# A hybrid encoder layer with experts: the first token tile's router and half of the first gather placed inside the output projection

## The chip, the cores and the metric

The kernel runs on one core of one Trainium2 chip. The metric is the device time of one execution in microseconds. In the code `pe` is TensorE, `dve` VectorE, `act` ScalarE, `pool` GpSimd, and `sp` the queue on SyncE that issues nearly all DMAs.

## What is computed

One encoder layer for 256 tokens of width 1024, all in float32. The first half mixes tokens (gated linear attention and softmax attention) and ends in an output projection; the second half sends every token to 4 of 32 experts. What matters here:

```python
h = h + concat([o_gla, o_att]) @ w_out                 # output projection, residual
n = rms_norm(h, ffn_norm_g)
logits = n @ w_router + b_router                       # 32 experts
top_val, top_idx = top_k(logits, 4); gates = softmax(top_val)
for each expert e, over the tokens that chose it:
    a = x_e @ w1[e] + b1[e]                            # w1[e]: 1024 x 2048
    act = min(a_glu, 7) * sigmoid(1.702 * a_glu) * (clip(a_lin, -7, 7) + 1)
    y += gate * (act @ w2[e] + b2[e])                  # w2[e]: 1024 x 1024
out = rms_norm(h + y, final_norm_g)
```

The weights of the experts are 32 x 12.58 MB = 403 MB; each is read once.

## The kernel before

**Tiles.** The 256 tokens are two tiles of 128 partitions (`t` = 0, 1); the residual `h` lies in SBUF as `h[:, t, 0:1024]`. An expert takes its tokens in a block of at most 64 (`CAP`). Which token goes to which place of the block is a 128 x 64 matrix per tile, `onehot[:, t, :]`, already scaled by the token's 1/rms. The expert's input `xg` must have the model dimension on the partitions.

**Order.** There is no scheduler: each engine runs its instructions in the order in which its block is written, and waits on semaphores (`S....`). Around the change the order is this.

1. The output projection on TensorE: `out_gla(t, nb, ks)` (L1456) is one 128x512 matmul per `k`, for tile `t` and half `nb` of the 1024 columns. When `k == 3` is done it counts `h_ps`. VectorE then adds the residual, `add_h(t, nb)` (L973, counts `h_done`), ScalarE squares the result for the norm (L590), and `turn_h(t, half)` (L1431) transposes the new `h` with four 128x128 turns, which VectorE or ScalarE copy into `hT` (L977, L595).
2. The router of a tile: `router_round(t, half)` (L1439, four 32-column matmuls each), a copy on ScalarE (L600), `router_sum(t)` (L1447), then on VectorE `choose(t)` (L990 to L995: logits, top values, the mask `chosen`), a matmul that counts places (L1501 for tile 0, L1506 for tile 1), and `first_mask(t)` (L1014, L1016), which writes `onehot[:, t, :]`.
3. The first gather, for expert 0: `first_gather(half, t)` (L1531) has `onehot` stationary (64 columns) and `h` moving (256 columns), two matmuls each. The rows that come out have the tokens on the partitions, so they are copied to SBUF (L1069 on VectorE for half 0, L617 on ScalarE for half 1), turned by `turn_first` (L1540) and multiplied by the norm's gain into `xg` (`half_out`, L1076). `keep_busy(n)` (L1487) is n matmuls whose result nobody reads.
4. The experts: TensorE multiplies `xg` by w1 (L1657, 8 matmuls per chunk of 2 MB, four chunks), then the activation, then w2 (L1701, two chunks). `start_hidden` (L1481) puts b1 into the accumulators.

**The weight ring.** SBUF has eight slots of 2 MB, plus three chunks that are loaded early elsewhere. A slot is refilled when TensorE has counted `chunk_used` for it. Slot 7 holds the projection's weights `w_out_gla` until all four `h_ps` are counted; its first chunk is issued after that (L345). So before expert 0 starts, everything that can be loaded has been loaded, and the next load waits for expert 0's first chunk.

The order of TensorE in the last part of the projection is written out by hand:

```python
out_gla(1, 0, range(4))
turn_h(0, 0)
turn_h(0, 1)
out_gla(1, 1, range(3))
turn_h(1, 0)
out_gla(1, 1, range(3, 4))
```

Of the kernel before, what the change touches and what calls it, by code (L numbers as in the profile page):

```python
# [120 lines left out]
def encoder_layer(nc, x, w_in, w_out, w_router, w1, b1, w2, b2, gate_w, columns, rows, final_g,  # L121
                  c_keep, c_front, later, split, out):
    ctx = ExitStack()
    with ctx:
# [28 lines left out]
        class Carve:  # L153
# [113 lines left out]
            onehot_ready onehot_first half_gathered half_rows half_turned half_xg gathered rows_done turned_ps xg_ready glu_ready sig_ready hid_ready combined  # L267
# [202 lines left out]
        def _(act):  # L470
# [133 lines left out]
            turned_out(0, 1, 1)  # L604
            square(1, 0)
            turned_out(1, 0, 7)
            router_parts(0)
# [7 lines left out]

            act.wait_ge(S.gathered, 1)
            nc.scalar.activation(rows_sb[:, SEQ:2 * SEQ], bank[6][:, 0:SEQ], ACT.Copy).then_inc(S.rows_done, 1)  # L617
# [68 lines left out]
        def _(dve):  # L686
# [313 lines left out]
            add_h(0, 0)  # L1000
            add_h(0, 1)
            mean_square(0)
            add_h(1, 0)
            turned_out(0, 0, 0)
            add_h(1, 1)
            turned_out(1, 1, 4)
            mean_square(1)
            dve.wait_ge(S.marks, 2)
            choose(0)
            choose(1)  # L1010

            def first_mask(t):
# [5 lines left out]
                    .then_inc((S.onehot_first, S.onehot_ready)[t], 1)  # L1018

# [39 lines left out]
            def gathered_out(n):  # L1059

                dve.wait_ge(S.turned_ps, n + 1)
# [5 lines left out]
            def half_rows_out():  # L1067
                dve.wait_ge(S.half_gathered, 1)
                nc.vector.tensor_copy(rows_sb[:, 0:SEQ], bank[3][:, 0:SEQ]).then_inc(S.half_rows, 1)  # L1069

            def half_out(half, b):

                n = KD // 2
                runs = W1_RUN // GROUPS
                dve.wait_ge((S.half_turned, S.turned_ps)[half], 1)
                nc.vector.tensor_tensor(xg[:, half * n * CAP:(half + 1) * n * CAP].rearrange("p (j r c) -> p j r c", j=GROUPS, c=CAP),  # L1076
                                        bank[b][:, SEQ:2 * SEQ].rearrange("p (r j c) -> p j r c", j=GROUPS, c=CAP),
                                        ffn_pairs[:, half * n:(half + 1) * n].rearrange("p (j r o) -> p j r o", j=GROUPS, o=1)
                                        .broadcast_to([P, GROUPS, runs, CAP]), ALU.mult).then_inc((S.half_xg, S.xg_ready)[half], 1)
# [91 lines left out]
        def _(pe):  # L1171
# [313 lines left out]
            def keep_busy(n):  # L1485
                for _ in range(n):
                    mm(bank[3][:, 0:P], ident, h[:, 0, 0:P], start=True, stop=True)  # L1487
# [285 lines left out]
```

## Time and profile before

| | us |
|---|---|
| median of 3 runs | 1052.62 |
| lowest and highest | 1050.64, 1052.72 |
| span of the profiled execution | 1047.4 |

The page and the answers of the trace show one profiled execution. PE is TensorE's matmuls, PEld its loads of stationary operands (a float32 matmul has two records of each, a turn has one), SPq the queue on SyncE. In the page's part on groups the columns are: line, engine, operation, written tile<-read tiles, shapes, count, then busy time and mean ns of one, then idle time ahead and what ended it. A row by stage has the stretch, its length, the busy time of PE, PEld, VectorE, ScalarE and GpSimd with counts, the granted TensorE clock (1.00 is 2.4 GHz, 0.50 is 1.2 GHz), the busy share of the DMA engines and GB/s. A row of the chain of work that ended last, or of the timeline, starts with its start and its length in us; in a PE row of either, the length reaches to the end of the last of the merged matmuls.

TensorE is busy for 1002.2 us of the span, VectorE for 223.0, ScalarE for 133.0; the DMA engines moved 421.48 MB at a mean of 402 GB/s.

### The profile page before, as it was taken

To read this page: it belongs to the slowest core of one execution; us is meant where nothing else is said; L and a number is where in the kernel's file an instruction comes from. 1 tells how busy PE (TensorE), PEld (TensorE's weight loads), DVE (VectorE), ACT (ScalarE), POOL (GpSimd) and SP (SyncE) were. 2 spreads that over 40 slices of the span, in tenths; PEclk is the share of its full clock that TensorE was granted. 3 is DMA by queue.
4 is the path that set the end of the run, shared out by engine and by line. 5 is a ranking of instruction groups with operands and counts; after the bars stand their busy time and mean duration, and the time that the engine had idled before them with its cause. 6 is when DMAs were issued, how large, how long until landed. Compare 5 with 4: busy or idle time off the path is not lost.

```text
span 1047.4 us, 11293 instructions
## 1 busy us (share of the span) xinstructions
PE 1002.2 (96%) x4739; PEld 429.8 (41%) x4739; DVE 223.0 (21%) x519; ACT 133.0 (13%) x262; POOL 13.4 (1%) x18
## 2 busy tenths in 40 slices
PE   8999999999999999989999989899999999999996
PEld 7646444444444444433343433333333333443332
DVE  5385331111111111111111111011111111110112
ACT  1154121111100000111110100011111010010112
POOL 0010100000000000000000000000000000000000
PEclk9999999999999999999999999999999999999999
DMA  9927969999999999999999999999999999999995
GB/s 356 283 80 316 407 254 430 427 428 430 425 427 428 427 429 425 429 433 432 434 429 432 427 435 426 436 430 430 432 430 437 427 437 430 425 427 428 428 423 224
DMA packets 26964, 421.48 MB, mean 402 GB/s; under 512 B 4368, under 2 KB 4752, under 8 KB 6864
## 3 DMA queue, kind: packets, MB, share of 16 engines
q1 hardware_dynamic: 26640, 420.68, 95.3%
q8 instruction: 29, 0.48, 0.2%
q10 hardware_dynamic: 288, 0.27, 0.1%
q14 instruction: 7, 0.06, 0.0%
HBM read 419.89 MB, written 1.05 MB: 402 GB/s over the span
## 4 chain that ended last, share of the span: by engine, by line
PE 68%; DMA 28%; DVE 1%; ACT 1%; POOL 0%; issue 0%; SPq 0%; DVEq 0%
PE bank L1657 30%; DMA ring<-in_w_dram 27%; PE bank L1701 15%; PE bank L1569 4%; PE bank L1550 3%; PE bank L1213 2%; PE bank L1683 1%; PE bank L1456 1%; PE bank L1287 1%; DMA ring<-in_w_in_dram 1%; PE bank L1384 1%; PE bank L1558 1%; PE bank L1481 1%; PE bank L1617 1%; PE bank L1256 1%; PE bank L1692 0%
## 5 line engine op out<-in xcount | busy, mean ns | idle before, releaser
L1657 PE MATMUL bank<-ring,work 128*64 128x512 f32 x2000 | 453.9, 606 | 30.9 <-DMA ring<-in_w_dram 30.9
L1657 PEld LDWEIGHTS bank<-ring,work 128*64 128x64 f32 x2000 | 175.1, 138 | 289.6 <-issue 235.0
L1701 PE MATMUL bank<-ring,work 128*64 128x512 f32 x992 | 219.7, 595 | 0.2
L1092 DVE TENSOR_SCALAR work<-bank 128x512 f32<-128x512 f32 x31 | 21.5, 692 | 641.7 <-PE bank L1657 641.7
L1701 PEld LDWEIGHTS bank<-ring,work 128*64 128x64 f32 x992 | 68.7, 137 | 129.4 <-issue 124.5
L627 ACT ACTIVATE bank<-work 128x512 f32<-128x512 f32 x31 | 18.6, 601 | 496.7 <-DVE work L1092 496.7
L1569 PE MATMUL bank<-work 64*128 64x512 f32 x256 | 63.6, 615 | 0.7 <-ACT work L664 0.7
L1550 PE MATMUL bank<-h,work 128*64 128x512 f32 x248 | 60.0, 593 | 0.0
L640 ACT ACTIVATE work<-bank 128x512 f32<-128x512 f32 x31 | 18.5, 597 | 214.5 <-PE bank L1701 214.5
L1569 PEld LDWEIGHTS bank<-work 64*128 64x128 f32 x256 | 22.0, 186 | 41.8 <-issue 40.2
L1062 DVE TENSOR_TENSOR work<-bank,ffn_pairs 128x512 f32<-128x512 f32 x31 | 21.5, 692 | 72.3 <-PE bank L1558 72.3
L1550 PEld LDWEIGHTS bank<-h,work 128*64 128x64 f32 x248 | 23.5, 137 | 30.0 <-issue 30.0
L1683 PEld LDWEIGHTS bank<-ckeep,work 128*128 128x128 f32 x124 | 17.3, 209 | 24.7 <-DVE work L1098 23.2
L622 ACT ACTIVATE work<-bank 128x512 f32<-128x512 f32 x31 | 18.5, 597 | 46.8 <-DVE work L1098 43.6
L1683 PE MATMUL bank<-ckeep,work 128*128 128x128 f32 x124 | 23.2, 309 | 1.1 <-DVE work L1098 1.1
L632 ACT ACTIVATE work<-bank 128x512 f32<-128x512 f32 x31 | 18.5, 597 | 28.9 <-PE bank L1683 28.8
L440 POOL TENSOR_TENSOR stat<-stat 128x1 f32<-128x1 f32 (+2 forms) x8 | 9.7, 1212 | 964.7 <-DVE stat L696 940.2
L1095 DVE SCALAR_TENSOR_TENSOR work<-work 128x512 f32<-128x512 f32 x31 | 21.4, 692 | 1.1
L1098 DVE TENSOR_TENSOR work<-work,bank 128x512 f32<-128x512 f32 x31 | 21.3, 686 | 1.1
L1093 DVE TENSOR_SCALAR work<-bank 128x512 f32<-128x512 f32 x31 | 21.1, 681 | 0.0
L1481 PE MATMUL bank<-biases,sel 96*64 96x512 bf16 x128 | 20.0, 389 | 0.0
L1558 PE MATMUL bank<-ckeep,work 128*128 128x128 f32 x124 | 20.0, 284 | 0.0
(217 smaller groups left out, 520.7 us busy)
## 6 DMA issues: line engine op xcount, KB each, us to landing
ring<-in_w_dram SPq DMA_DIRECT2D x48, 4096.0 KB, 29.8
ring<-in_w_dram SPq DMA_DIRECT2D x90, 2048.0 KB, 20.2
ring<-in_w_in_dram SPq DMA_DIRECT2D x8, 1168.0 KB, 17.5
ring<-in_w_dram SPq DMA_DIRECT2D x6, 1024.0 KB, 34.1
work<-in_w_dram SPq DMA_DIRECT2D x2, 2048.0 KB, 14.7
ring<-in_w_out_dram SPq DMA_DIRECT2D x2, 1024.0 KB, 11.0
ring<-in_w_out_dram SPq DMA_DIRECT2D x1, 2048.0 KB, 17.2
h<-in_x_dram SPq DMA_DIRECT2D x2, 512.0 KB, 3.7
```

The lines of the kernel that those rows point to most:

```text
L1062: nc.vector.tensor_tensor(xg.rearrange("p (h r c) -> p h r c", h=GROUPS, c=CAP), bank[2][:, :].rearrange("p (r h c) -> p h r c", h=GROUPS, ...
L1092: nc.vector.tensor_scalar(glu, bank[2][:, :], LIMIT, None, ALU.min).then_inc(S.glu_ready, 1)
L1093: nc.vector.tensor_scalar(lin, bank[5][:, :], LIMIT, -LIMIT, ALU.min, ALU.max).then_inc(S.dve_step, 1)
L1095: nc.vector.scalar_tensor_tensor(lin, lin, 1.0, glu, ALU.add, ALU.mult).then_inc(S.dve_step, 1)
L1098: nc.vector.tensor_tensor(lin, lin, bank[2][:, :], ALU.mult).then_inc(S.hid_ready, 1)
L1481: mm(bank[(2, 5)[g]][j * CAP:(j + 1) * CAP, :], sel, of_group(b1_parts, g, j), start=True, stop=False, skip_group_check=True)
L1550: last = mm(bank[6][j * CAP:(j + 1) * CAP, :], onehot[:, t, :], h[:, t, j * 512:(j + 1) * 512], start=t == 0, stop=t == TILES - 1, skip_gr ...
L1558: last = nc.tensor.transpose(bank[2][:, r * P:(r + 1) * P], apart[:, :, r], ident)
L1569: last = mm(bank[Y[i]][:, :], gatedT[j * CAP:(j + 1) * CAP, t, :], res[j * CAP:(j + 1) * CAP, :], start=start, stop=stop, skip_group_check ...
L1657: last = mm(bank[(2, 5)[g]][j * CAP:(j + 1) * CAP, :], xg[:, k * CAP:(k + 1) * CAP], of_group(row_of(chunk, r, 2 * FF), g, j), start=False ...
L1683: last = nc.tensor.transpose(bank[5][:, r * P:(r + 1) * P], apart[:, :, r], ident)
L1701: last = mm(bank[6][j * CAP:(j + 1) * CAP, :], hidT[:, r, s * CAP:(s + 1) * CAP], row_of(chunk, r, D)[:, j * 512:(j + 1) * 512], start=s = ...
```

## The change

Tile 0's router no longer waits for the end of the projection. On TensorE, `turn_h(0, ...)` goes ahead of the last two matmuls of `out_gla(1, 0)`; `router_round(0, ...)`, `router_sum(0)`, `turn_h(1, 0)` and the counting matmul of tile 0 go between the four matmuls of `out_gla(1, 1)`. VectorE and ScalarE are reordered to match: `choose(0)` and `first_mask(0)` stand ahead of `add_h(1, 1)`.

The first gather is written the other way round: `h` (every fourth column, 128 of them) is stationary and `onehot` (64 columns) moves, four matmuls in place of two for each half and tile. Its result has the model dimension on the partitions already, so both copies (L1069, L617) and both `turn_first` (L1540) are gone. Tile 0's two parts stand inside tile 1's router, around `turn_h(1, 1)`; tile 1's two parts stand directly ahead of expert 0. All six `keep_busy` matmuls are gone.

```diff
@@ -602,9 +602,9 @@
             square(0, 0)
             square(0, 1)
             turned_out(0, 1, 1)
+            router_parts(0)
             square(1, 0)
             turned_out(1, 0, 7)
-            router_parts(0)
             square(1, 1)
             router_parts(1)
...
                     .then_inc(S.wexp_done, 1)
-
-            act.wait_ge(S.gathered, 1)
-            nc.scalar.activation(rows_sb[:, SEQ:2 * SEQ], bank[6][:, 0:SEQ], ACT.Copy).then_inc(S.rows_done, 1)
 
             def rows_out(n):
                 act.wait_ge(S.gathered, n + 1)
@@ -997,18 +994,6 @@
...
             dve.wait_ge(S.pairs_in, 16 * W1_RUN * W1_RUN)
-            add_h(0, 0)
-            add_h(0, 1)
-            mean_square(0)
-            add_h(1, 0)
-            turned_out(0, 0, 0)
-            add_h(1, 1)
-            turned_out(1, 1, 4)
-            mean_square(1)
-            dve.wait_ge(S.marks, 2)
-            choose(0)
-            choose(1)
-
...
+            add_h(0, 0)
+            add_h(0, 1)
+            turned_out(0, 0, 0)
+            mean_square(0)
+            add_h(1, 0)
+            dve.wait_ge(S.marks, 2)
+            choose(0)
+            first_mask(0)
+            add_h(1, 1)
+            turned_out(1, 1, 4)
+            mean_square(1)
+            choose(1)
+            first_mask(1)
...
-            def half_rows_out():
-                dve.wait_ge(S.half_gathered, 1)
-                nc.vector.tensor_copy(rows_sb[:, 0:SEQ], bank[3][:, 0:SEQ]).then_inc(S.half_rows, 1)
-
             def half_out(half, b):
 
                 n = KD // 2
-                runs = W1_RUN // GROUPS
-                dve.wait_ge((S.half_turned, S.turned_ps)[half], 1)
-                nc.vector.tensor_tensor(xg[:, half * n * CAP:(half + 1) * n * CAP].rearrange("p (j r c) -> p j r c", j=GROUPS, c=CAP),
-                                        bank[b][:, SEQ:2 * SEQ].rearrange("p (r j c) -> p j r c", j=GROUPS, c=CAP),
-                                        ffn_pairs[:, half * n:(half + 1) * n].rearrange("p (j r o) -> p j r o", j=GROUPS, o=1)
-                                        .broadcast_to([P, GROUPS, runs, CAP]), ALU.mult).then_inc((S.half_xg, S.xg_ready)[half], 1)
+                dve.wait_ge((S.half_gathered, S.gathered)[half], 1)
+                nc.vector.tensor_tensor(xg[:, half * n * CAP:(half + 1) * n * CAP].rearrange("p (r c) -> p r c", c=CAP),
+                                        bank[b][:, 0:n * CAP].rearrange("p (r c) -> p r c", c=CAP),
+                                        ffn_pairs[:, half * n:(half + 1) * n].rearrange("p (r o) -> p r o", o=1)
+                                        .broadcast_to([P, n, CAP]), ALU.mult).then_inc((S.half_xg, S.xg_ready)[half], 1)
...
-            first_mask(0)
-            first_mask(1)
-            half_rows_out()
             half_out(0, 3)
+            half_out(1, 6)
             tables()
-            half_out(1, 6)
...
             pe.wait_ge(S.glaT_v, 1)
             out_gla(0, 0, range(4))
             out_gla(0, 1, range(4))
-            pe.wait_ge(S.glaT_a, 1)
-            out_gla(1, 0, range(4))
-            turn_h(0, 0)
-            turn_h(0, 1)
-            out_gla(1, 1, range(3))
-            turn_h(1, 0)
-            out_gla(1, 1, range(3, 4))
-
...
 
+            def first_gather(half, t):
+
+                if half == 0:
+                    pe.wait_ge((S.onehot_first, S.onehot_ready)[t], 1)
+                apart = h[:, t, half * 512:(half + 1) * 512].rearrange("p (m r) -> p m r", r=W1_RUN)
+                for r in range(W1_RUN):
+                    last = mm(bank[(3, 6)[half]][:, r * CAP:(r + 1) * CAP], apart[:, :, r], onehot[:, t, :],
+                              start=t == 0 and r == 0, stop=t == TILES - 1, skip_group_check=True)
+                if t == TILES - 1:
+                    last.then_inc((S.half_gathered, S.gathered)[half], 1)
+
+            pe.wait_ge(S.glaT_a, 1)
+            out_gla(1, 0, range(2))
+            turn_h(0, 0)
+            turn_h(0, 1)
+            out_gla(1, 0, range(2, 4))
             pe.wait_ge(S.wr_done, 1)
-            def keep_busy(n):
-                for _ in range(n):
-                    mm(bank[3][:, 0:P], ident, h[:, 0, 0:P], start=True, stop=True)
-
             router_round(0, 0)
             router_round(0, 1)
+            out_gla(1, 1, range(1))
+            router_sum(0)
+            out_gla(1, 1, range(1, 3))
+            turn_h(1, 0)
+            pe.wait_ge(S.chosen_done, 1)
+            mm(bank[1][:, 0:EXPERTS], before_b, chosen[:, 0, :], start=True, stop=True).then_inc(S.rank_ps, 1)
+            out_gla(1, 1, range(3, 4))
             router_round(1, 0)
+            first_gather(0, 0)
             turn_h(1, 1)
-            router_sum(0)
-            keep_busy(2)
+            first_gather(1, 0)
             router_round(1, 1)
             router_sum(1)
             start_hidden(0)
-
-
-            pe.wait_ge(S.chosen_done, 1)
-            mm(bank[1][:, 0:EXPERTS], before_b, chosen[:, 0, :], start=True, stop=True).then_inc(S.rank_ps, 1)
-            pe.wait_ge(S.hT_a, 2)
+            pe.wait_ge(S.hT_v, 2)
             mm(bank[7][:, 0:EXPERTS], ones_b, chosen[:, 0, :], start=True, stop=False)
             mm(bank[4][:, 0:EXPERTS], ones_b, chosen[:, 0, :], start=True, stop=False)
             pe.wait_ge(S.chosen_done, 2)
...
-            RUNS = W1_RUN // GROUPS
-
-            def first_gather(half, t):
-                if half == 0 and t == 0:
-                    keep_busy(4)
-                pe.wait_ge((S.onehot_first, S.onehot_ready)[t], 1)
-                for j in range(GROUPS):
-                    last = mm(bank[(3, 6)[half]][j * CAP:(j + 1) * CAP, 0:RUNS * P], onehot[:, t, :],
-                              h[:, t, half * 512:(half + 1) * 512].rearrange("p (m r) -> p m r", r=W1_RUN)[:, :, j * RUNS:(j + 1) * RUNS], start=t == 0, stop=t == TILES - 1, skip_group_check=True)
-                if t == 1:
-                    last.then_inc((S.half_gathered, S.gathered)[half], 1)
-
-            def turn_first(half):
-                pe.wait_ge((S.half_rows, S.rows_done)[half], 1)
-                apart = rows_sb[:, half * RUNS * P:(half + 1) * RUNS * P].rearrange("p (m r) -> p m r", r=RUNS)
-                for r in range(RUNS):
-                    last = nc.tensor.transpose(bank[(3, 6)[half]][:, (RUNS + r) * P:(RUNS + r + 1) * P], apart[:, :, r], ident)
-                last.then_inc((S.half_turned, S.turned_ps)[half], 1)
...
-                    if first and c == 0:
-                        turn_first(1)
                     if first and c == 1:
...
-            first_gather(0, 0)
             first_gather(0, 1)
-            first_gather(1, 0)
-            turn_first(0)
             first_gather(1, 1)
```

The `first_gather` of the diff is used for expert 0 alone; the later gathers stay as they were. Two waits of the later experts count one less, since the first gather no longer counts `rows_done` and `turned_ps`.

TensorE's order from the last matmuls of the projection to expert 0's first chunk, before (L1456 is the projection, L1431 the turns, L1439 and L1447 the router, L1487 the unread matmuls, L1531 the gather, L1540 `turn_first`, L1657 expert 0):

```order
127 L1456 MATMUL bank<-ring,work 128x512 x3
128 L1431 MATMUL bank<-ckeep,h 128x128 x4
129 L1456 MATMUL bank<-ring,work 128x512
130 L1439 MATMUL bank<-work,wr_sb 32x128 x12
131 L1431 MATMUL bank<-ckeep,h 128x128 x4
132 L1447 MATMUL bank<-ckeep,work 128x32
133 L1487 MATMUL bank<-h,ckeep 128x128 x2
134 L1439 MATMUL bank<-work,wr_sb 32x128 x4
```

And now (L1447 is here the projection, L1422 the turns, L1430 and L1438 the router, L1491 the counting matmul, L1473 the gather):

```order
127 L1447 MATMUL bank<-ring,work 128x512 x2
128 L1430 MATMUL bank<-work,wr_sb 32x128 x8
129 L1447 MATMUL bank<-ring,work 128x512
130 L1438 MATMUL bank<-ckeep,work 128x32
131 L1447 MATMUL bank<-ring,work 128x512 x2
132 L1422 MATMUL bank<-ckeep,h 128x128 x4
133 L1491 MATMUL bank<-work,ckeep 128x32
134 L1447 MATMUL bank<-ring,work 128x512
135 L1430 MATMUL bank<-work,wr_sb 32x128 x4
136 L1473 MATMUL bank<-work,h 128x64 x4
137 L1422 MATMUL bank<-ckeep,h 128x128 x4
138 L1473 MATMUL bank<-work,h 128x64 x4
```

Eight narrow router matmuls, the router's sum and the count moved ahead of the projection's last matmul, and four gather matmuls ahead of the last turn (row 137).

TensorE's last rows ahead of expert 0's first chunks, before:

```order
143 L1531 MATMUL bank<-h,work 64x256 x6
144 L1540 MATMUL bank<-ckeep,work 128x128 x2
145 L1531 MATMUL bank<-h,work 64x256 x2
146 L1657 MATMUL bank<-ring,work 64x512 x8
147 L1540 MATMUL bank<-ckeep,work 128x128 x2
148 L1657 MATMUL bank<-ring,work 64x512 x8
```

And now (L1504, L1505 count tile 1's places, L1636 is expert 0):

```order
144 L1504 MATMUL bank<-work,ckeep 128x32
145 L1505 MATMUL bank<-work,ckeep 128x32
146 L1473 MATMUL bank<-work,h 128x64 x8
147 L1636 MATMUL bank<-ring,work 64x512 x16
148 L1510 MATMUL bank<-ckeep,work 128x128 x2
```

The turns between gather and expert are gone, and eight gather matmuls with 128 stationary columns stand where eight with 64 stood.

## Rows read from the trace of the kernel before

**Rows 1.** The page: the profiled span, and the costliest group.

```profile
span 1047.4 us, 11293 instructions
...
L1657 PE MATMUL bank<-ring,work 128*64 128x512 f32 x2000 | 453.9, 606 | 30.9 <-DMA ring<-in_w_dram 30.9
```

**Rows 2.** By stage: two stretches of the experts.

```profile
260.00:500.00 240.00, 235.59 (x1114) 95.96 (x1112) 40.46 (x90) 24.00 (x45) 0.00 (x0) 0.99 1.01 428
...
750.00:1000.00 250.00, 234.98 (x1090) 92.70 (x1088) 36.67 (x82) 21.98 (x42) 0.00 (x0) 0.98 1.00 429
```

**Rows 3.** The chain of work that ended last: two early experts, first DMA piece.

```profile
186.29 7.07 PE bank L1701 x32
...
212.62 7.07 PE bank L1701 x32
...
437.71 30.85 DMA ring<-in_w_dram
```

**Rows 4.** By stage, 1 us each: where the DMA engines stop and resume.

```profile
138.00:139.00 1.00, 1.00 (x12) 0.56 (x8) 0.02 (x1) 0.00 (x0) 0.00 (x0) 1.00 0.64 270
139.00:140.00 1.00, 0.92 (x8) 0.42 (x6) 0.40 (x1) 0.00 (x0) 0.00 (x0) 1.00 0.00 0
...
144.00:145.00 1.00, 1.00 (x6) 0.52 (x6) 0.27 (x1) 0.00 (x0) 0.00 (x0) 1.00 0.00 0
145.00:146.00 1.00, 1.00 (x8) 0.41 (x5) 0.92 (x9) 0.00 (x0) 0.00 (x0) 1.00 1.00 213
```

**Rows 5.** The chain of work that ended last, 115 to 150 us.

```profile
131.21 0.86 PE bank L1456 x2
132.07 0.79 PE bank L1439 x24
132.86 0.66 PE bank L1431 x4
...
134.29 0.47 PE bank L1439 x8
...
137.87 1.08 PE bank L1531 x8
...
139.46 0.51 PE bank L1540 x2
...
140.57 3.62 PE bank L1657 x16
```

**Rows 6.** Timeline, 131 to 142 us: the same stretch by instruction.

```profile
132.10 0.69 DVE L973 TENSOR_TENSOR h<-bank,h 128x512 f32<-128x512 f32 x1 [3.46 <-PE bank L1456]
...
133.54 0.69 DVE L977 COPY work<-bank 128x512 f32<-128x512 f32 x1 [0.75 <-PE bank L1431]
...
135.56 0.25 DVE L990 SCALAR_TENSOR_TENSOR work<-bank,stat,work 128x32 f32<-128x32 f32 x1
...
137.19 0.31 DVE L1016 TENSOR_SCALAR work<-ckeep,work,stat 128x64 f32<-128x64 f32 x1
...
138.98 0.42 DVE L1069 COPY work<-bank 128x256 f32<-128x256 f32 x1 [1.47 <-PE bank L1531]
...
140.00 0.42 DVE L1076 TENSOR_TENSOR work<-bank,ffn_pairs 128x256 f32<-128x256 f32 x1 [0.60 <-PE bank L1540]
```

**Rows 7.** Timeline: loads of stationary operands, 32 columns, 128 together, 128 strided.

```profile
132.00 0.59 PEld L1439 LDWEIGHTS bank<-work,wr_sb 128*32 128x32 f32 x24 [0.76 <-issue]
...
136.71 0.97 PEld L1487 LDWEIGHTS bank<-h,ckeep 128*128 128x128 f32 x8
...
185.54 0.56 PEld L1558 LDWEIGHTS bank<-ckeep,work 128*128 128x128 f32 x4
```

**Rows 8.** By stage, 1 us each: the granted clock around short and long idle stretches.

```profile
136.00:137.00 1.00, 0.59 (x9) 0.47 (x8) 0.89 (x8) 0.89 (x3) 0.00 (x0) 1.00 0.92 393
...
467.00:468.00 1.00, 0.00 (x0) 0.00 (x0) 0.00 (x0) 0.00 (x0) 0.00 (x0) 1.00 0.99 426
...
469.00:470.00 1.00, 1.00 (x4) 0.24 (x2) 0.00 (x0) 0.00 (x0) 0.00 (x0) 0.50 0.84 360
```

More of the change, by code:

```diff
@@ L266, in encoder_layer @@
             parts_ps part_sb_done logit_ps top_done wexp_done chosen_done rank_ps count_ps tables_done gateT_ps gateT_sb extra_done
-            onehot_ready onehot_first half_gathered half_rows half_turned half_xg gathered rows_done turned_ps xg_ready glu_ready sig_ready hid_ready combined
+            onehot_ready onehot_first half_gathered half_xg gathered rows_done turned_ps xg_ready glu_ready sig_ready hid_ready combined
             gated_ready gatedT_ps gatedT_sb hidT_ps hidT_sb res_ready chunk_used
@@ L1059, in gathered_out @@
             def gathered_out(n):
-                dve.wait_ge(S.turned_ps, n + 1)
+                dve.wait_ge(S.turned_ps, n)
                 nc.vector.tensor_tensor(xg.rearrange("p (h r c) -> p h r c", h=GROUPS, c=CAP),
@@ L1554, in turn_rows @@
             def turn_rows(n):
-                pe.wait_ge(S.rows_done, n + 1)
+                pe.wait_ge(S.rows_done, n)
                 apart = rows_sb.rearrange("p (m r) -> p m r", r=W1_RUN)
```

## The prediction

> **What bounds the kernel now.** First the page. TensorE is busy 96% of the span, and the group of expert matmuls has 30.9 us of idle time ahead of it, all put down to the DMA of weights [rows 1]. The share hides which of the two limits, so next come the stages: from 260 to 500 us and from 750 to 1000 us the DMA engines are full (shares 1.01 and 1.00) at 428 and 429 GB/s [rows 2]. An expert's 12.58 MB at 429 GB/s take 29.3 us. TensorE needs less: in the chain two early experts stand 212.62 - 186.29 = 26.33 us apart, without a wait [rows 3]. So the DMA engines are the slower of the two by 3.0 us an expert; TensorE lives on what was loaded ahead until 437.71 us, where the chain first passes through a transfer [rows 3].
>
> The span is therefore the moment at which the DMA engines start to work without a break, plus the rest of the weights at 429 GB/s, plus a tail. That moment is in the rows of 1 us: the transfers end between 138 and 139 us, there are none from 139 to 145, and they are full again in the row from 145 [rows 4]. The ring is full and waits for expert 0's first chunk to be used. The chain says when: the chunk's matmuls start at 140.57 and take 3.62, to 144.19 us [rows 5]; the first bytes come about 1 us later. From then on a chunk takes 2.1 MB / 429 GB/s = 4.9 us to load and about 4.1 us to use, so the queue stays fed. **What the change is worth is how much earlier or later expert 0's first chunk is used, and nothing else**; TensorE's savings behind that point only make it wait longer for the ring.
>
> **The path to that point, before.** The projection's last matmul ends at 132.06 [rows 5]; add at 132.10; turn at 132.86; copy at 133.54; router matmuls at 134.29; logits on VectorE at 135.56; tile 1's `onehot` is done at 137.19 + 0.31 = 137.50 [rows 5, 6]. This chain is tile 1's router. Tile 0's runs beside it and is not in it. Then: gather from 137.8, copy at 138.98, turn at 139.46, gain at 140.00, and the chunk starts at about 140.5 [rows 5, 6]. So 5.4 us from the projection to the mask, and 3.0 us from the mask to the chunk.
>
> **Mask to chunk, after.** The copy (0.42), the turn (0.51) and their handovers go, and so does the wait for the last unread matmuls (137.50 to 137.80). In their place stand eight gather matmuls of tile 1, so 16 records, ahead of the chunk. Their moving operand has 64 columns, their stationary one 128, strided by four. No row shows that form. From below: 128 stationary columns that lie together follow each other every (0.97 - 0.19) / 7 = 0.111 us [rows 7], where 0.19 is the length of one load. The nearest row is the later experts' turn, whose stationary operand is 128 columns strided by four: (0.56 - 0.21) / 3 = 0.117 us [rows 7]. From above I take twice the plain pitch, 0.22, since that row is a turn and has one record per operand, not two. I choose 0.12, by the turn: 16 x 0.12 = 1.92 us, and with 0.06 for the start the chunk begins 1.98 us after the mask. The other branch is shorter: half of the gather (0.96), 0.33 until VectorE sees it, the gain 0.42, 0.06 to TensorE, 1.8 in all; so the matmuls themselves set it, and VectorE's second `half_out` hides beneath the first two chunks. Gain: 3.0 - 2.0 = **1.0 us**.
>
> The Trainium skill, "TensorE: Matmul & The Clock Gate", section "LDWEIGHTS", makes the load a matter of columns alone, columns / 1.2 ns, which is an estimate of 107 ns for 128 columns whatever their stride; the strided row's 0.117 us is above that. By the rule the 16 records would take 1.71 us and the gain would be 1.2 us.
>
> **Projection to mask, after.** Here the change puts work in front of tile 1's chain.
> - Ahead of the projection's last matmul: 16 records of the narrow router at (0.59 - 0.11) / 23 = 0.021 us [rows 7], so 0.34, and an estimated 0.1 to start them; the router's sum, two records, 0.22; the count, about 0.1. Together 0.8 us. The turns and projection matmuls only change places. Nothing waits there: tile 0's logits come at about 129.8, tile 1's took 1.94 us to the finished mask with the count in it (135.56 to 137.50) [rows 6], and TensorE reaches tile 0's count at 131.7. So `h_ps` comes at 132.9, VectorE's add starts there, free since `first_mask(0)` ended near 132.5.
> - Ahead of tile 1's last turn: `router_round(1, 0)`, 0.3, and four gather matmuls, 8 x 0.12 = 0.96. TensorE has issued the projection at 132.7 and reaches the turn at 134.0. The add would allow it at 132.9 + 0.8 = 133.7. So the turn starts at 134.0, where it started at 132.86.
> - The second part of tile 0's gather (0.96) stands behind the turn, where TensorE waits for VectorE's copy anyway: 134.4 to 135.4, and the copy hands over at 134.0 + 0.69 + 0.69 + 0.06 = 135.4. Hidden, but with nothing to spare.
> - Behind that all is as before and moved by the same amount: the mask is done at 137.50 + 1.15 = 138.65. Loss: **1.15 us**. The gain chain of VectorE and GpSimd for the 1/rms is moved too and ends about 0.3 us ahead of the logits.
>
> SyncE's load into slot 7 waits for `h_ps` and is issued 0.8 us later; its transfer ends near 139.5 instead of 138.7, still 4.5 us ahead of the next one. Behind it on that queue stands only the load that waits for the first chunk. Cost: nothing.
>
> **The sum.** 1.15 - 1.0 = +0.15 us: the chunk starts at 140.65 instead of 140.5 and is used at 144.3. The turn taken out behind the first chunk (0.44) helps TensorE alone. The profiled span would go from 1047.4 to 1047.6. The runs are 5.2 us above the span in the median, and that stays: 1052.62 + 0.15 = **1052.8 us**.
>
> **Rivals.**
> - *Tile 1's router isn't pushed back, or the gather goes at its moving columns.* If the four gather matmuls ahead of the turn took 0.5 us (64 of the 128 columns per record) the turn would wait for VectorE alone, at 133.7, and the last 16 records would take 0.9. VectorE's branch would then set the chunk, 1.35 us behind the mask: 138.3 + 1.35 = 139.7, a gain of 0.8; without the 0.8 us in the projection too it would be 1.6. Against it: both rows with 128 stationary columns have 0.11 or more. Time 1051.0 to 1051.8. Chance 0.2.
> - *The strided load is slow.* At 0.22 a record the turn waits until 134.8, the second part of the gather pushes the next router matmuls to 136.9 (2.6 us later than before), and the last 16 records take 3.5: the chunk starts at 143.7, 3.2 us later. The sum turns to slower as soon as a record takes more than 0.115. Time 1055.8; halfway, at 0.16, 1054.1. Chance 0.1.
> - *The clock falls.* The twelve records of unread matmuls are gone and TensorE idles three times for 0.6 us or so between 135.5 and 138.7. Before, the row at 136 us has 0.59 us busy and a full clock; a fall came only behind a longer stop: the row at 467 us is empty, and the row at 469 has 0.50 [rows 8]. No stretch of that kind arises here, which speaks against it. If it falls, the first chunk takes up to twice its 3.62 us: +1.7 to +3.6 us, 1054.5 to 1056.4. Chance 0.12. The Trainium skill's page "TensorE: Matmul & The Clock Gate", section "A second HAM failure mode: psum-queue depth-cycling", says that short idles between groups can be enough to throttle; the 1.00 at 136 us disagrees here.
> - *What bounds is elsewhere*, so that the first chunk's time moves nothing: 1052.6, inside the forecast.
>
> **How the numbers follow.** A measurement of this kernel can tell about 0.2% (2.1 us) from no change; the three runs of before span 2.08 us by themselves. Forecast 0.55; gather by moving columns 0.2; slow load 0.1; clock 0.12; the rest 0.03. Slower by over 0.2% are half of the clock case, a third of the slow load, and scatter, 0.13 in all; faster only the far end of the first rival with scatter, 0.05; within 0.2% is 0.82. Range: from the fastest run of before with a gain of 0.6, 1050.0, to the middle of the slow cases, 1055.1.
>
> **What would show it.** In the profile after: the DMA engines resume at 145 us, give or take 0.5; the mask near 138.7 and the chunk near 140.7; tile 1's last turn near 134.0, behind the gather; 16 strided records in 1.9 us; clock 1.00 from 130 to 145 us; idle time before expert matmuls put down to DMA a little larger. Wrong would be: a mask at 137.5 or earlier, a chunk started well before 140 us, a clock of 0.50 near 140, or a span that moves by another amount than the first chunk does.

## The result

| | median us | runs | ratio to before | 95% interval |
|---|---|---|---|---|
| before | 1051.78 | 4 | 1 | |
| changed | 1055.83 | 4 (1054.54 to 1055.90) | 1.0045 | 1.0032 to 1.0057 |

The change makes the kernel slower by 4 to 5 us: the medians lie 4.05 us apart, and the ratio, which is worked out from the runs and not from the two medians, gives 4.7 us (3.4 to 6.0). I had forecast 1052.8 us and no measurable change. The profiled execution's span went from 1047.4 to 1052.8 us. The page after, span and costliest group (in the changed kernel L1636 is the expert matmul, L1447 the projection, L1430 the router's matmuls, L1422 the turns of `h`, L1473 the new gather):

```profile
span 1052.8 us, 11283 instructions
...
L1636 PE MATMUL bank<-ring,work 128*64 128x512 f32 x2000 | 456.6, 610 | 29.7 <-DMA ring<-in_w_dram 29.7
```

TensorE's idle time for weights hardly moved (30.9 us in [rows 1]), so the loss isn't in the experts' steady part. The stages of 1 us show where it is; they answer [rows 4]:

```profile
139.00:140.00 1.00, 0.66 (x7) 0.16 (x4) 0.82 (x6) 0.99 (x3) 0.00 (x0) 0.60 0.56 238
...
150.00:151.00 1.00, 1.00 (x7) 0.35 (x5) 0.00 (x0) 0.00 (x0) 0.00 (x0) 1.00 0.00 0
151.00:152.00 1.00, 1.00 (x8) 0.50 (x5) 0.00 (x0) 0.00 (x0) 0.00 (x0) 1.00 0.82 180
```

The DMA engines stop about 1 us later than before (the row from 139 us still has 238 GB/s) and resume in the row from 151 us, not in the one from 145. The load that waits for the first chunk is issued at 144.22 us before and at 150.77 us after (SyncE's queue in the timeline, before first, then after):

```profile
144.22 4.40 SPq L345 DMA_DIRECT2D ring<-in_w_dram  x2
```

```profile
150.77 0.33 SPq L345 DMA_DIRECT2D ring<-in_w_dram  x1
```

I call the issue of this load the **restart** and count it from the start of the last part of the projection (116.78 us before, 116.66 after), since that start itself differs between profiles by up to 4 us for reasons ahead of the change. Before it is 144.22 - 116.78 = 27.44 us, after 150.77 - 116.66 = 34.11: **6.67 us later**. The chain of work that ended last shows what fills them; it answers [rows 5]:

```profile
133.05 0.36 PE bank L1430 x8
133.41 2.01 PE bank L1473 x8
135.42 0.44 PE bank L1422 x4
135.86 1.81 PE bank L1473 x8
137.67 0.40 PE bank L1430 x8
...
140.82 3.99 PE bank L1473 x16
144.82 9.38 PE bank L1636 x32
```

Eight records of the gather take 2.0 us, not 0.96, and sixteen take 4.0, not 1.92. The two parts that I had placed as free, around tile 1's last turn, are now in the chain: the turn starts at 135.42 (132.86 before), the next router matmuls at 137.67 (134.29). And the first two chunks take 9.38 us together, where one takes 3.62 at the full clock [rows 5]. The granted clock says why:

```profile
141.00:142.00 1.00, 1.00 (x5) 1.00 (x6) 0.00 (x0) 0.52 (x1) 0.00 (x0) 0.50 0.00 0
...
149.00:150.00 1.00, 1.00 (x6) 0.46 (x4) 0.00 (x0) 0.00 (x0) 0.00 (x0) 0.78 0.00 0
```

From 139.2 to 149.4 us TensorE ran at 1.2 GHz (worked out from the rows at 139 and 149 us, which are part one level and part the other); before, it had 2.4 GHz there. So two of my rivals came true together. Of the 6.67 us, 4.37 lie ahead of the first chunk, which starts 28.16 us behind the projection's start and not 23.79, and 2.30 in the chunk itself: from its start to the next load it is 5.95 us, not 3.65.

### The profile page after: what moved, and what is told of

Its sections match the earlier page's. It is cut to its first block, busy times and chain, and to the rows that moved or that the text cites. A ratio compares the mean times of both kernels' runs of the same rounds, so it can differ in the third digit from the quotient of the medians.

```text
span 1052.8 us, 11283 instructions
## 1 busy us (share of the span) xinstructions
PE 1009.3 (96%) x4739; PEld 436.7 (41%) x4739; DVE 222.9 (21%) x518; ACT 132.7 (13%) x261; POOL 13.4 (1%) x18
## 4 chain that ended last, share of the span: by engine, by line
PE 69%; DMA 27%; DVE 1%; ACT 1%; POOL 0%; issue 0%; SPq 0%; DVEq 0%
PE bank L1636 31%; DMA ring<-in_w_dram 27%; PE bank L1678 15%; PE bank L1548 4%; PE bank L1529 3%; PE bank L1204 3%; PE bank L1660 1%; PE bank L1447 1%; PE bank L1278 1%; PE bank L1375 1%; PE bank L1537 1%; PE bank L1464 1%; PE bank L1473 1%; PE bank L1596 1%; PE bank L1247 1%; DMA ring<-in_w_in_dram 1%
## 5 line engine op out<-in xcount | busy, mean ns | idle before, releaser
L1636 PE MATMUL bank<-ring,work 128*64 128x512 f32 x2000 | 456.6, 610 | 29.7 <-DMA ring<-in_w_dram 29.7
L1636 PEld LDWEIGHTS bank<-ring,work 128*64 128x64 f32 x2000 | 176.5, 139 | 290.1 <-issue 237.8
```

Source lines behind the costliest of these rows:

```text
L1636: last = mm(bank[(2, 5)[g]][j * CAP:(j + 1) * CAP, :], xg[:, k * CAP:(k + 1) * CAP], of_group(row_of(chunk, r, 2 * FF), g, j), start=False ...
```

## The experiments

My first theory: the loss has two causes. One is the load of a stationary operand that is read with a stride; the other is the clock. Rivals: the new form is slow even without a stride; the new order costs by itself; the clock fell because the unread matmuls are gone, or because the slow gather leaves the array idle. Restarts are counted as above, "+" is against the 27.44 us of before. Medians of each group are in the text; ratios are to the kernel before on the same chip and, as above, not exactly the quotients of the medians. The code cuts leave out the parts of an edit that only keep the rest of the program in step.

### Without the stride

```diff
-                apart = h[:, t, half * 512:(half + 1) * 512].rearrange("p (m r) -> p m r", r=W1_RUN)
+                apart = h[:, t, half * 512:(half + 1) * 512].rearrange("p (r m) -> p m r", r=W1_RUN)
```

> The changed kernel with the first gather's stationary operand read as 128 columns that lie together in place of every fourth column (so expert 0 gets the wrong columns of h; work and order are the same). Theory 'stride': the record pitch falls from 0.24 to 0.11-0.12 us, tile 1's last turn starts near 134.1 (was 135.25), the mask is done near 138.7 (140.8), the first chunk starts near 140.8 (144.75). Rival 'two records with 64 moving columns are slow in themselves': pitch stays 0.24 and all those times stay. For the clock: if it fell because the unread matmuls are gone it is still 0.50 near 140-145 us and the DMA engines resume near 147.3 (time about +2.2 us on before); if it fell because the slow gather leaves the array idle it is 1.00 and they resume near 145.4 (time within 0.5 us of before).

Measured: 1051.68 us against 1049.07, ratio 1.0021 (1.0011 to 1.0030); restart 147.69 - 116.77 = 30.92, +3.48 us. The first chain row is a quarter of the gather at the full clock, the second is tile 1's two quarters:

```profile
133.52 1.03 PE bank L1473 x8
...
138.98 3.67 PE bank L1473 x16
```

```profile
138.00:139.00 1.00, 0.23 (x3) 0.13 (x3) 0.61 (x3) 0.98 (x3) 0.00 (x0) 0.77 0.92 393
139.00:140.00 1.00, 1.00 (x5) 1.00 (x5) 0.00 (x0) 0.69 (x1) 0.00 (x0) 0.50 0.64 270
```

At the full clock the stride was the whole cost of a record: 2.01 us for eight became 1.03. But the clock still fell, at 138.5 us, and at 0.50 a record without a stride takes 3.67 / 16 = 0.23 us. So the stride explains the first half of the loss (the restart goes from +6.67 to +3.48), and the clock doesn't need it.

### The unread matmuls back

```diff
             router_round(1, 1)
+            keep_busy(2)
             router_sum(1)
...
+            keep_busy(4)
             first_gather(0, 1)
             first_gather(1, 1)
```

> The changed kernel with the six unread matmuls back: two ahead of router_sum(1), four ahead of first_gather(0, 1). Theory 'the clock fell because they are gone': clock 1.00 throughout, the first chunk takes 3.6 us in place of 5.5, the DMA engines resume near 149.5 in place of 151.3, time 1.7 us below the changed kernel, 2.3 to 3 above before. Rival 'the clock fell because the slow gather leaves the array idle': still 0.50 from about 139 to 149 us, time as the changed kernel or up to 0.5 above it.

Measured: 1055.07 against 1049.07, ratio 1.0060 (1.0044 to 1.0077); restart 150.32 - 116.78 = 33.54, +6.10. The clock stayed full to the end of the gather at 144.98 us and fell 0.4 us behind it:

```profile
139.00:140.00 1.00, 0.67 (x6) 0.13 (x4) 0.90 (x6) 0.99 (x2) 0.00 (x0) 1.00 0.64 270
...
141.00:142.00 1.00, 1.00 (x7) 1.00 (x6) 0.00 (x0) 0.63 (x1) 0.00 (x0) 1.00 0.00 0
...
146.00:147.00 1.00, 1.00 (x4) 0.26 (x2) 0.89 (x8) 0.00 (x0) 0.00 (x0) 0.50 0.00 0
```

With the strided gather the unread matmuls save 0.6 us at most: the fall only comes later, in the first chunk. Neither of my two expectations for the clock came out, since it was neither full throughout nor low from 139 us on.

### The order alone, and the form alone

The changed kernel's order with the old form of the gather (`onehot` stationary, copy, turn), without unread matmuls:

```diff
+                for j in range(GROUPS):
+                    last = mm(bank[(3, 6)[half]][j * CAP:(j + 1) * CAP, 0:RUNS * P], onehot[:, t, :],
...
-                apart = h[:, t, half * 512:(half + 1) * 512].rearrange("p (m r) -> p m r", r=W1_RUN)
```

> The changed kernel's order with the first gather in its old form (onehot stationary, copy, turn, gain). Theory 'the form costs, the order costs little': h_ps as in the changed kernel (133.1), the turn starts near 133.9, the mask is done near 138.5, the first chunk starts near 140.9, used at 144.6 if the clock stays at 1.00: time +0.5 us on before; +2.3 if the clock falls. Rival 'the order is what costs': the first chunk starts at 143 or later with the old form too.

Measured: 1052.08 against 1049.07, ratio 1.0024 (1.0015 to 1.0034); restart 147.36 - 116.75 = 30.61, +3.17. The mask of tile 1 is done at 138.62 us, 1.12 later than before. The rest is the clock: the first chunk takes 5.43 us.

```profile
141.90 5.43 PE bank L1653 x16
```

```profile
144.00:145.00 1.00, 1.00 (x4) 0.23 (x1) 0.00 (x0) 0.00 (x0) 0.00 (x0) 0.50 0.00 0
```

The kernel before with the new form only, in its old order, its unread matmuls kept:

```diff
-                    last = mm(bank[(3, 6)[half]][j * CAP:(j + 1) * CAP, 0:RUNS * P], onehot[:, t, :],
...
+                    last = mm(bank[(3, 6)[half]][:, r * CAP:(r + 1) * CAP], apart[:, :, r], onehot[:, t, :],
```

> The kernel before in its old order, with unread matmuls, and only the first gather in its new form. Mask at 137.5 as before; then 32 records. Theory 'stride': 32 x 0.24 = 7.7 us, the first chunk starts near 145.6, the DMA engines resume near 150.3 with a full clock: time +5.0 us on before. Rival (my prediction's pitch of 0.12): 3.9 us, the chunk starts at 141.8, time +1.3.

Measured: 1054.46 against 1049.07, ratio 1.0056 (1.0039 to 1.0072); restart 150.89 - 116.73 = 34.16, +6.72. All 32 records stand in the chain, at 7.46 / 32 = 0.233 us each, and the clock falls in the middle of them, at 142.4 us, though unread matmuls stand directly ahead:

```profile
137.83 7.46 PE bank L1523 x32
145.29 9.03 PE bank L1642 x32
```

```profile
140.00:141.00 1.00, 1.00 (x6) 1.00 (x5) 0.00 (x0) 0.00 (x0) 0.00 (x0) 1.00 0.00 0
...
142.00:143.00 1.00, 1.00 (x6) 1.00 (x6) 0.00 (x0) 0.00 (x0) 0.00 (x0) 0.69 0.07 16
...
144.00:145.00 1.00, 1.00 (x6) 1.00 (x5) 0.00 (x0) 0.00 (x0) 0.00 (x0) 0.50 0.00 0
```

Here TensorE counts as busy in every row from 137 us on, and loads stationary operands throughout the gather, and the clock falls all the same.

### The load by itself

Batches of unread matmuls at the kernel's start, each 16 records, behind 24 warming ones:

```diff
+            def by(r, n=P):
+                return h0.rearrange("p (m r) -> p m r", r=r)[:, 0:n, 0]
+            for _ in range(8):
+                mm(bank[0][:, 0:64], h0[:, 0:P], ones[:, 0:64], start=True, stop=True)
+            for _ in range(8):
+                mm(bank[0][:, 0:64], by(2), ones[:, 0:64], start=True, stop=True)
+            for _ in range(8):
+                mm(bank[0][:, 0:64], by(4), ones[:, 0:64], start=True, stop=True)
...
```

> The changed kernel with batches of unread matmuls at its start, behind 24 warming ones: 8 float32 matmuls each (16 records) with 128 stationary columns that lie together, every 2nd, every 4th, every 8th; then 64 stationary columns together and every 4th; then every 4th with 128 and with 256 moving columns; then 16 turns with the operand together and every 4th. Theory 'a strided stationary operand loads at half speed in a matmul, not in a turn': pitch 0.11-0.12 together, 0.24 at every stride from 2 on, 0.06 and 0.12 for 64 columns, 0.24 with 128 and with 256 moving columns, 0.11 and 0.12 for the turns. Rival 'only a stride of 16 bytes or more is slow': every 2nd stays at 0.12.

The loads, in order: 128 columns together; every 2nd; 4th; 8th; 64 columns together and every 4th; every 4th with 128 and with 256 moving columns; turns, together and every 4th (timeline, start and length of the batch):

```profile
13.63 1.87 PEld L1193 LDWEIGHTS bank<-work,h 128*128 128x128 f32 x16
15.42 1.96 PEld L1195 LDWEIGHTS bank<-work,h 128*128 128x128 f32 x16
17.30 3.81 PEld L1197 LDWEIGHTS bank<-work,h 128*128 128x128 f32 x16
21.02 3.90 PEld L1199 LDWEIGHTS bank<-work,h 128*128 128x128 f32 x16
25.04 1.78 PEld L1201 LDWEIGHTS bank<-work,h 128*64 128x64 f32 x16
26.70 2.02 PEld L1203 LDWEIGHTS bank<-work,h 128*64 128x64 f32 x16
28.83 3.81 PEld L1205 LDWEIGHTS bank<-work,h 128*128 128x128 f32 x16
32.55 3.83 PEld L1207 LDWEIGHTS bank<-h 128*128 128x128 f32 x16
36.28 1.90 PEld L1209 LDWEIGHTS bank<-ckeep,h 128*128 128x128 f32 x16
38.15 2.01 PEld L1211 LDWEIGHTS bank<-ckeep,h 128*128 128x128 f32 x16
```

The granted clock has to be read beside these lengths:

```profile
17.00:18.00 1.00, 1.00 (x8) 1.00 (x8) 0.00 (x0) 0.00 (x0) 0.00 (x0) 1.00 0.98 400
18.00:19.00 1.00, 1.00 (x6) 1.00 (x6) 0.00 (x0) 0.00 (x0) 0.00 (x0) 0.89 0.98 402
...
22.00:23.00 1.00, 1.00 (x6) 1.00 (x6) 0.00 (x0) 0.00 (x0) 0.00 (x0) 0.50 1.02 430
...
34.00:35.00 1.00, 1.00 (x6) 1.00 (x6) 0.00 (x0) 0.00 (x0) 0.00 (x0) 1.00 1.09 190
```

At the full clock a matmul's 128 columns cost 0.12 us a record when they lie together or when every second is taken, and 0.24 us at every 4th, also with 128 and 256 moving columns. **The turn is indifferent**: 0.12 with and without the stride, both at the full clock. That is the row that I had gone by. My expectation said that every 2nd would be slow; there the rival, "only 16 bytes or more", was right.

The clock fell in this run too, at 18.8 us, 1.5 us into the first batch of every 4th column, with TensorE busy in every row from 5 us on. It came back at 29.0 us, as the batch with 128 moving columns had begun, and with 128 and 256 moving columns the same stride kept the full clock for the 7 us up to 36 us. So the stride alone isn't what brings the clock down; here it fell only with 64 moving columns. This is one profile. So the batch of every 8th and both batches of 64 columns ran at 0.50. There 128 columns that lie together cost 0.23 us a record as well (e1_contig), so the 0.24 of every 8th doesn't show a cost of that stride, and the two batches of 64 columns (0.11 together, 0.13 at every 4th) say nothing of them at the full clock.

### Both causes taken away

The changed kernel's order and form, with the model dimension stored in another order so that the stationary columns lie together (`x`, `w_in`, `w_out`, the router and the gains permuted alike, and the gain loaded in one piece, not in 16; the turns of the later experts read columns that lie together too), and the unread matmuls back:

```diff
+    apart = np.arange(D).reshape(2, P, W1_RUN).transpose(0, 2, 1).reshape(-1)
...
-        "x": np.asarray(x)[0],
+        "x": np.asarray(x)[0][:, apart],
...
-                apart = h[:, t, half * 512:(half + 1) * 512].rearrange("p (m r) -> p m r", r=W1_RUN)
+                apart = h[:, t, half * 512:(half + 1) * 512].rearrange("p (r m) -> p m r", r=W1_RUN)
```

> The changed kernel's order and form, with the model dimension stored in another order (x, w_in, w_out, the router and the gains permuted alike), so that the first gather's 128 stationary columns lie together, and with the six unread matmuls back. Theory 'two causes, stride and clock': pitch 0.12, mask near 138.8, first chunk near 140.9, clock 1.00 to the end of the first chunk, DMA engines resume near 145.5: time within 0.5 us of before. If the unread matmuls don't hold the clock even with the quick gather: 0.50 in the first chunk, resume near 147.5, time +2 us.

Measured: 1050.27 against 1051.15, ratio 0.9988 (0.9979 to 0.9998); restart 148.68 - 120.69 = 27.99, +0.55. The clock stays full through the gather and the first chunks:

```profile
143.28 1.73 PE bank L1469 x16
145.01 7.07 PE bank L1638 x32
```

```profile
145.00:146.00 1.00, 1.00 (x7) 0.44 (x8) 0.88 (x4) 0.00 (x0) 0.00 (x0) 1.00 0.06 16
```

The mask of tile 1 is done at 142.84 us, 22.15 behind the projection's start where before has 20.72: +1.43. The chunk starts 2.17 us behind the mask in place of 3.07: -0.90. Together that is +0.53, where my sum was 1.15 - 1.0 = +0.15. The ratio is a little below 1 although the restart is 0.55 us later. The kernel differs from before in the early loads and the later turns as well, so I don't read a gain of the change into it.

The order alone with the unread matmuls back; the edit to e3_order is that of e2_unread:

> The changed kernel's order with the old form of the gather, as in e3_order, and the six unread matmuls back. Theory 'in e3_order 1.1 us was the order and the rest the clock': clock 1.00 through the first chunk, mask near 138.6, chunk started near 141.2 and used near 144.9, DMA engines resume near 145.8: time +0.7 us on before, 2.3 below e3_order. Rival 'the order alone costs 3 us': the resume stays near 148.

Measured: 1051.47 against 1050.78, ratio 1.0007 (0.9997 to 1.0017); restart 145.31 - 117.13 = 28.18, +0.74. The first chunk takes the usual time, at a full clock:

```profile
141.67 3.62 PE bank L1658 x16
```

```profile
141.00:142.00 1.00, 1.00 (x7) 0.40 (x8) 0.83 (x4) 0.29 (x1) 0.00 (x0) 1.00 0.00 0
```

The mask is done 1.15 us later than before and the chunk starts 0.75 us later. Next to e6_apart, the same order with the quick form (+0.53), this gives what the new form is worth when nothing slows it: 0.2 us.

### Only the unread matmuls taken out

```diff
             router_sum(0)
-            keep_busy(2)
...
-                if half == 0 and t == 0:
-                    keep_busy(4)
```

> The kernel before without its six unread matmuls, nothing else. Theory 'the clock fell because they are gone': the granted clock is 0.50 from about 137 us, the gather's records and the first chunk take longer, the DMA engines resume near 148 in place of 145.1, time +2.5 to +3 us. Rival 'the clock depends on the new gather and order alone': clock 1.00, time 0.3 us below before (the gather starts at 137.5 in place of 137.8).

Measured: 1050.31 against 1051.15, ratio 0.9988 (0.9975 to 1.0001); restart 146.52 - 118.58 = 27.94, +0.50. The clock does fall, at 139.7 us, but it is back at 143.1, with nearly all of the first chunk (142.75 to 146.49 us) at the full clock. Both of my expectations for the time were wrong: the unread matmuls hold the clock, but in the order of before that is worth 0.5 us in the profile and nothing that the runs can tell.

```profile
141.00:142.00 1.00, 1.00 (x6) 0.60 (x6) 0.27 (x1) 0.00 (x0) 0.00 (x0) 0.50 0.00 0
...
143.00:144.00 1.00, 1.00 (x6) 0.34 (x4) 0.26 (x2) 0.98 (x2) 0.00 (x0) 0.94 0.00 0
144.00:145.00 1.00, 1.00 (x7) 0.35 (x5) 0.00 (x0) 0.48 (x1) 0.00 (x0) 1.00 0.00 0
```

### Does the end follow the first chunk?

```diff
             first_gather(1, 1)
+            for _ in range(4):
+                mm(bank[1][:, :], ident, h[:, 0, 0:512], start=True, stop=True)
```

> The kernel before with four unread matmuls of 512 columns (3.4 us) directly ahead of expert 0's first chunk. Theory 'the end follows the first chunk one for one': the chunk starts at 143.9, the DMA engines resume near 148.6, time +3.4 us. Rival 'the ring has slack, the bound lies elsewhere': time within 0.5 us of before.

Measured: 1053.43 against 1050.78, ratio 1.0029 (1.0018 to 1.0041), which is 3.0 us (1.9 to 4.3); restart 147.88 - 116.80 = 31.08, +3.64; span 1051.0 against 1047.4, +3.6. One for one, within the scatter. The chain has the four unread matmuls (L1712) and, behind them, the chunk at its usual length:

```profile
140.59 3.63 PE bank L1712 x8
144.22 3.63 PE bank L1657 x16
```

### A better order

The order of before with the quick form, that is with the model dimension stored as in e6_apart: three quarters of the gather ahead of the first chunk, the last one behind it, and four unread matmuls in place of six. The cut is against the kernel before:

```diff
             first_gather(0, 0)
             first_gather(0, 1)
             first_gather(1, 0)
-            turn_first(0)
-            first_gather(1, 1)
...
                     if first and c == 0:
-                        turn_first(1)
+                        first_gather(1, 1)
```

> The order of before (router of tile 0 behind the projection, four of the six unread matmuls) with the quick new form of the gather: half 0 of both tiles, half 1 of tile 0, then the first chunk, and half 1 of tile 1 behind it. Mask of tile 1 at 137.5 as before; 24 records from 137.3 on at 0.12: the first chunk starts near 140.2 (140.5 before): time -0.3 us at a full clock. If the clock falls in the gather, the records take 0.23 and the chunk 5.5 us: resume near 148.5, time +3.4.

> The kernel of e7_late once more, with more rounds. The profile of its first run had the first chunk used 0.5 us before that of before at a full clock, its other runs scattered up to 1057. If the scatter was the chip's: ratio 0.999 to 1.000, time -0.3 to -0.5 us. If the clock or something else in this kernel falls in most runs: ratio 1.001 to 1.003 again, and the profile shows 0.50 near 140 us or a projection that starts later than 116.8.

The restart is 143.71 - 116.78 = 26.93 in the first and 143.84 - 116.90 = 26.94 in the second, 0.5 us earlier than before, at a full clock:

```profile
137.42 2.63 PE bank L1519 x24
140.04 3.63 PE bank L1639 x16
```

The times don't show it: ratios 1.0020 (1.0005 to 1.0035) and 1.0009 (0.9997 to 1.0021), runs from 1048.4 to 1057.5 us. In the first group the kernel is slower than before and its interval leaves out 1, in the second it doesn't. The mean granted clock was 0.987 to 0.991 in 21 of the 22 runs, and 0.983 in the one of 1057.5 us, so the clock isn't what scatters the others. A gain of 0.5 us is below what these runs can tell, and why they scattered more than before isn't settled. So no kernel here is measurably faster than before through the gather.

## Why the prediction was wrong

- **What bounds** was right. The end follows the first chunk: in e10_later the restart moves by 3.64 and the span by 3.6, and from the issue of the load that waits for the first chunk to the end of the span it is 901.8 to 904.6 us in all twelve profiles of these kernels. In the changed kernel that load is issued 6.55 us later by the clock of the trace (150.77 against 144.22) and the span grows by 5.4; the 1.2 us between them lie within that scatter.
- **From span to median** the prediction had a wrong reading: that the runs are 5.2 us above the span, and that this stays. A run of the kernel before or of the changed one takes about 1.7 us more than its own span (1054.54 against 1052.8 in the changed kernel), and the profiled execution of before was about 3.5 us shorter than the median run, an estimate from 5.2 - 1.7. The forecast loses nothing by this, since it adds its sum to the median, but spans and medians can't be compared directly. The 4.05 us between the medians rest on few runs that scatter by 2 us. Against the 19 runs of before in the first group of experiments, e2_unread and e4_form, whose restarts are 6.1 and 6.7 us later, are slower by 6.3 and 5.9 us by the ratio.
- **Projection to mask, +1.15 us**: near, where nothing slows the gather. In the form that I had forecast but without the stride (e1_contig) the turn starts at 134.55, where I had 134.0, and the mask is 1.44 us later. The 1.12 us with the old gather (e3_order) are no confirmation, since its first quarter takes 0.60 us and not 0.96. With the stride the step fails: the first quarter holds the turn until 135.42, and the second, which I had called hidden with nothing to spare, pushes the next router matmuls to 137.67. The mask came 3.3 us later than before.
- **The pitch of 0.12 us** is the step that failed. It was taken from a turn, as the nearest row with a stride of four, between bounds of 0.11 and 0.22. The turn isn't slowed by the stride; the matmul pays double. Even my upper bound was a little low: a record took 0.23 to 0.25 us. In the sum: 16 records took 4.0 us in place of 1.9, and each quarter ahead about 1 us more. The rival "the strided load is slow", with a restart 3.2 us later, had the mechanism; the chunk starts 4.4 us later. That its 1055.8 us are the measured median is luck: its restart is less than half of the 6.67 us.
- **The clock**, chance 0.12, was the second failure, and cost 2.3 us within the first chunk. I had compared with a fall behind a stop without any matmul [rows 8] and found no such stop in the new order. The runs show that no stop is needed. Two things were enough, each without the other: no unread matmuls, with TensorE idle for at most 0.64 us at a time (e1_contig, e3_order, and e8_no_unread in the old order), and the strided gather itself with the unread matmuls in place. In e4_form TensorE is busy in every row from 137 us to the fall at 142.4, in m1_forms from 5 us to 18.8; in e2_unread it idles in the rows from 139 and 140 us and is busy for the 4 us ahead of the fall. Only with both taken away does the clock stay full (e6_apart, e9_order_unread). By the rule of the Trainium skill that I had cited against the row at 136 us, "TensorE: Matmul & The Clock Gate", section "A second HAM failure mode: psum-queue depth-cycling", short idles are enough: the traces of e3_order (0.50 in the row from 139 us) and e8_no_unread (0.50 in the row from 140 us) agree, and the row at 136 us had unread matmuls around it. Whether it is the idles or the narrow matmuls around them that let the clock fall there, no run separates.
- **The two together.** Restart: neither +0.55 (e6_apart), no unread matmuls +3.48 (e1_contig), stride +6.10 (e2_unread), both +6.67 (changed kernel). They don't add up, since the strided gather brings a fall of the clock with it.
- **The copy and the turn that were removed** gave back 0.90 us from mask to chunk in e6_apart, where I had 1.0, although four unread matmuls hold its gather back there. But the old form in the new order gives back 0.40 as well (e9_order_unread: mask +1.15, chunk +0.75), because tile 0's half is already gathered, and its quarters ahead of the turn are shorter. Net the new form is worth 0.2 us, and order and form together leave the chunk 0.5 us later than before.
- **The load into slot 7** cost nothing: issued at 133.08, its transfer ended before 140 us, eleven microseconds ahead of the next.

What stays open: how much of the fall in e2_unread comes from the strided records and how much from the wait ahead of them, and why removing the unread matmuls costs 2.4 us (e9_order_unread to e3_order) to 2.9 (e6_apart to e1_contig) in the new order but 0.5 in the old one. The clock was low from 139.7 to 143.1 us in e8_no_unread, nearly all of it ahead of the first chunk, and from 138.5 to 145.4 in e1_contig, half of the chunk included; no run separates when it returns from where the gather stands. e6_apart has the same waits and unread matmuls as e2_unread and no fall, so the waits alone aren't enough.

## What to carry to other kernels

Look at how the stationary operand is read before swapping operands to save a copy: at the full clock 128 float32 columns with a stride of four cost twice the columns that lie together, and a turn with the same stride doesn't show it. When unread matmuls go out, or records with few moving columns come in ahead of the work on the path, read the granted clock up to the end of that work, not only where the idles are. And when work is moved into a gap "with nothing to spare", price the case in which it is twice as long: here the router matmuls behind it started at 137.67 us, where I had 135.4.

## What the runs showed of the hardware that I had not expected

- Float32 stationary operand of a matmul, 128 columns, full clock: 0.12 us a record together and at every second element, 0.24 at every fourth; a turn 0.12 together and at every fourth (m1_forms). A stride of eight was measured at 0.50 alone.
- A gather record's time depends on the clock almost only without the stride: 16 records together took 1.73 us at the full clock (e6_apart) and 3.67 at 0.50 (e1_contig); strided they took 3.68 at the full clock (e2_unread) and 3.99 at 0.50 (changed kernel).
- The clock can fall from 1.00 to 0.50 while the rows by stage show TensorE busy for 1.00 us of each us (e4_form, 137 to 145 us; m1_forms, 5 to 20 us).
